# Dense attention's first key and query tiles placed among the branch tiles of the two-map attention, merged chunks stored one by one, buffers laid out anew

## The reference, cut to what matters

```
u = rms_norm(h)
qa, ka, va, qb, kb, vb, ga, gb = split(u @ w_in)
oa = rms_norm((softmax(q1 k1) - lam * softmax(q2 k2)) va)        # two-map attention, branch a
qh = axial_rope(rms_norm(qb)); kh = axial_rope(rms_norm(kb))     # dense attention, branch b
ob = softmax(qh kh) vb                                           # 8 query heads, 2 key heads
merged = sigmoid(ga) * (oa @ w_branch_a) + sigmoid(gb) * (ob @ w_branch_b)
h = h + merged @ w_out
```

## Time and profile before

| | us |
|---|---|
| median of 3 runs | 3543.96 (3541.33 to 3544.52) |
| the profiled execution, its own time | 3540.61 |
| its span, first to last instruction | 3538.8 |
| PE busy | 3312.3 (94% of the span) |
| DVE busy | 1410.5 (40%) |
| ACT busy | 1013.9 (29%) |
| POOL busy | 801.9 (23%) |
| PE, share of the chain that ended last | 52% |

### The profile page before, as it was taken

The page is one execution under the profiler, slowest core; times in us unless marked ns, Lnnn a source line. Parts: engine busy times, 40 slices in busy tenths (PEclk is TensorE's granted clock), DMA queues, the critical chain, the costliest instruction groups (busy, mean ns, idle before and its releaser), DMA issues.

```text
span 3538.8 us, 52696 instructions
## 1 busy us (share of the span) xinstructions
PE 3312.3 (94%) x20576; PEld 2907.5 (82%) x20576; DVE 1410.5 (40%) x2478; ACT 1013.9 (29%) x1873; POOL 801.9 (23%) x513
## 2 busy tenths in 40 slices
PE   7999988999999998999999889899999999879996
PEld 5677766888887887898989689889898999679996
DVE  4555543000002545666666630255545134432222
ACT  3433331000001213554555520145444210300001
POOL 3111133333332333122111123201000123012221
PEclk9999999999999998999999999999999999989998
DMA  4011122111112112000000001300000121458986
GB/s 148 31 31 31 31 73 84 48 46 45 46 46 96 48 48 91 19 19 21 24 20 19 13 24 47 109 17 25 27 25 19 53 98 59 171 194 307 316 309 238
DMA packets 75339, 275.50 MB, mean 78 GB/s; under 512 B 10736, under 2 KB 15600, under 8 KB 74400
## 3 DMA queue, kind: packets, MB, share of 16 engines
q1 hardware_dynamic: 67952, 234.08, 19.4%
q0 software_dynamic: 5632, 17.04, 2.0%
q10 hardware_dynamic: 1584, 22.07, 1.5%
HBM read 229.49 MB, written 38.34 MB: 76 GB/s over the span
## 4 chain that ended last, share of the span: by engine, by line
PE 52%; DVE 4%; issue 3%; ACT 1%; DMA 1%; POOL 0%; SPq 0%; DVEq 0%; ACTq 0%; POOLq 0%
PE PS L555 13%; PE PS L2875 7%; PE PS L2475 6%; PE PS L543 5%; PE PS L2661 3%; PE PS L2539 3%; PE PS L2905 3%; PE PS L2737 3%; PE PS L2506 3%; PE PS L2702 3%; PE PS L2685 0%; PE PS L2540 0%; PE PS L2819 0%; PE PS L2738 0%; DMA part_b<-raw_b 0%
## 5 line engine op out<-in xcount | busy, mean ns | idle before, releaser
L577 POOL CAST w_hi<-ring 128x1024 fp32r<-128x1024 f32 x174 | 182.9, 1051 | 1919.0 <-PE PS L555 772.4
L579 POOL TENSOR_TENSOR w_lo<-ring,w_hi 128x1024 fp32r<-128x1024 f32 x174 | 436.2, 2507 | 14.0
L555 PE MATMUL PS<-u_hi,w_hi 128*128 128x512 f32 (+1 forms) x1256 | 351.2, 371 | 17.6 <-DVE u_lo L509 7.7
L555 PE MATMUL PS<-u_lo,w_hi 128*128 128x512 f32 (+1 forms) x1256 | 350.9, 370 | 0.0
L555 PE MATMUL PS<-u_hi,w_lo 128*128 128x512 f32 (+1 forms) x1256 | 348.3, 369 | 0.0
L555 PEld LDWEIGHTS PS<-u_hi,w_hi 128*128 128x128 f32 x1256 | 228.2, 190 | 56.3 <-issue 12.7
L555 PEld LDWEIGHTS PS<-u_hi,w_lo 128*128 128x128 f32 x1256 | 228.3, 189 | 37.5
L555 PEld LDWEIGHTS PS<-u_lo,w_hi 128*128 128x128 f32 x1256 | 228.6, 189 | 35.5
L1726 ACT ACTIVATE EA<-EA,small_sb 128x1040 f32<-128x1040 f32 x144 | 166.7, 1158 | 211.0 <-DVE small_sb L2075 211.0
L1204 DVE TENSOR_TENSOR hid<-sq,PS 128x1024 f32 x22 | 26.9, 1221 | 457.9 <-PE PS L555 457.9
L2075 DVE CUSTOM_DVE_ANT_0 EA<-PS,biasH,low_a 128x1024 f32<-128x1024 f32 x128 | 163.6, 1278 | 68.1 <-PE PS L2506 62.7
(11 more groups left out here) (406 smaller groups left out, 6740.8 us busy)
## 6 DMA issues: line engine op xcount, KB each, us to landing
ring<-in_stream SPq DMA_DIRECT2D x174, 512.0 KB, 3.6
w_gate_sb<-in_w_gate SPq DMA_DIRECT2D x64, 512.0 KB, 6.4
w_up_sb<-in_w_up SPq DMA_DIRECT2D x64, 512.0 KB, 8.1
w_down_sb<-in_w_down SPq DMA_DIRECT2D x64, 512.0 KB
x_keep<-xT ACTq DMA_DIRECT2D x2, 4176.0 KB, 12.9
xT<-x_keep ACTq DMA_DIRECT2D x1, 4176.0 KB, 13.4
x2T<-x_keep ACTq DMA_DIRECT2D x1, 4176.0 KB, 13.7
x_keep<-x2T SPq DMA_DIRECT2D x1, 4176.0 KB, 15.1
```

Source lines behind the costliest of these rows:

```text
L555: last = mm(bank(to_bank, width), w[j][:, c, :], src[:, c, b * width:(b + 1) * width], start=(c == 0 and k == 0), stop=(c == KD - 1 and k ...
L577: pool.tensor_copy(w_hi[j][:, :, :], w_raw[j][:, :, :]).then_inc(S["w_rounded"], 1)
L579: pool.tensor_tensor(w_lo[j][:, :, :], w_raw[j][:, :, :], w_hi[j][:, :, :], ALU.subtract).then_inc(S["w_split"], 1)
```

## The change

**Order.** Branch a stops after branch tile 3 and gate tile 5 (`AHEAD = 4`). The tiles K and Q run there. Then come branch tile 4, the query sums, gate 6, branch 5, gate 7, branch 6, branch 7, and only then V. The stream's layout, the tile numbers and SP's queue follow that order. The loops on the three engines run over four chunks; the rest is written out.

**Stores.** `gated` writes its product in place, over `gate_a`. ACT stores each chunk (522 KB) by itself when it is done, and the sigmoid of gate d waits until chunk d-2 has landed. The last waits are for all 8 chunks.

**Buffers.** The tables, `raw_b`, `part_b`, the squares, `q_f`, `k_f`, `k_hi` and `k_lo` lie behind the operands of branch a, so they can be written while that runs. `q_hi`, `q_lo`, `vTb`, `EB`, `Vb` and `PTb` lie over those operands and are written after branch tile 7. The tables load early, when the turned output is out of its buffer. K's thirds go to banks 6, 7, 3, its sums to 4, 5, 4, Q's thirds to 0, 1, 2, and the first query sums to bank 7.

```diff
+AHEAD = 4
+FIRST0 = MG0 + 2 * AHEAD + 2
...
         def item_tile(g, x):
-            return B0 + g * ITEMS + x
+            return FIRST0 + x if g == 0 and x < VALUES else B0 + g * ITEMS + x
...  (SP)
-                pairs(A0 + 2, B0 + 2)
-                sp.wait_ge(S["w_used"], tile_done(B0 - 1))
+                pairs(A0 + 2, FIRST0 + 2)
+                sp.wait_ge(S["as_t"], 2 * (NT + 1))
                 sp.dma_start(cos[:, :], A["cos"]).then_inc(S["rope_ld"], 16)
                 sp.dma_start(sin[:, :], A["sin"]).then_inc(S["rope_ld"], 16)
+                for x in (KEYS, FIRST):
+                    swapped(0, x)
+                pairs(FIRST0 + 4, item_tile(0, VALUES) + 2)
...  (ACT)
-                act.wait_ge(S["mg_ma"], KD + CREDIT)
-                act.dma_start(m_keep, mergedT[:, :, :]).then_inc(S["m_st"], 16)
+                def keep(d, j):
+                    act.wait_ge(S["mg_ma"], d + 1 + CREDIT)
+                    act.dma_start(m_keep[:, bass.ds(d, 1), :].rearrange("p a n -> p (a n)"), gate_a[j][:, :]).then_inc(S["m_st"], 16)
+                def next_gate(d, j, late=0):
+                    keep(d - 2, j)
+                    act.wait_ge(S["m_st"], 16 * (d - 1))
+                    sigmoid(d, j, gate_tile(d, late), 0)
+                with act.Fori(1, AHEAD // 2 + 1) as i:
+                    for j in range(2):
+                        next_gate(2 * i + j, j)
                 for c in range(3):
                     wait_unit(0, KEYS, c)
-                    rope_raw(0, KEYS, c, c)
+                    rope_raw(0, KEYS, c, (6, 7, 3)[c])
                 for c in range(3):
-                    key_root(0, c, (6, 7, 6)[c])
+                    key_root(0, c, (4, 5, 4)[c])
                     wait_unit(0, FIRST, c)
-                    rope_raw(0, FIRST, c, 3 + c)
-                act.wait_ge(S["m_st"], 16)
+                    rope_raw(0, FIRST, c, c)
+                split_keys(0)
+                query_root(0, 0)
+                for d in range(AHEAD + 2, KD):
+                    next_gate(d, d % 2, 1)
+                keep(KD - 2, 0)
+                act.wait_ge(S["w_used"], tile_done(B0 + 1))
+                split_queries(0, 0)
+                keep(KD - 1, 1)
...  (DVE)
-                    dve.tensor_tensor(mergedT[...], thirds(gate_a[j][:, :]), banks(3, 3, CH), ALU.mult)
+                    dve.tensor_tensor(thirds(gate_a[j][:, :]), thirds(gate_a[j][:, :]), banks(3, 3, CH), ALU.mult)
...
                 query_recip(0, 0)
-                dve.wait_ge(S["m_st"], 16)
+                for d in range(AHEAD, KD - 1):
+                    gated(d, d % 2, branch_tile(d, 1))
+                gated(KD - 1, 1, B0 + 1)
                 lower_queries(0, 0)
                 meta_scores(0, 0)
+                scores_b(0)
+                dve.wait_ge(S["m_st"], 16 * KD)
...  (PE)
+                with pe.Fori(0, AHEAD) as d:
+                    branch_a(d, 0, branch_tile(d))
+                    gate_a_tile(d + 2)
+                pe.wait_ge(S["mg_ma"], AHEAD + CREDIT)
                 for c in range(3):
-                    whole_unit(0, KEYS, c, c)
-                pe.wait_ge(S["mg_ma"], KD + CREDIT)
+                    whole_unit(0, KEYS, c, (6, 7, 3)[c])
+                pe.wait_ge(S["mg_sa"], AHEAD + 2)
                 for c in range(3):
                     if c == 2:
                         pe.wait_ge(S["ob_ksd"], 1)
-                    key_sums(0, c, (6, 7, 6)[c])
-                    whole_unit(0, FIRST, c, 3 + c)
+                    key_sums(0, c, (4, 5, 4)[c])
+                    whole_unit(0, FIRST, c, c)
                 pe.wait_ge(S["ob_ksd"], 3)
+                branch_a(AHEAD, 0, branch_tile(AHEAD, 1))
+                query_sums(0, 0)
+                gate_a_tile(AHEAD + 2, 1)
+                for d in range(AHEAD + 1, KD - 1):
+                    branch_a(d, 0, branch_tile(d, 1))
+                    if d + 2 < KD:
+                        gate_a_tile(d + 2, 1)
+                branch_a(KD - 1, 1, B0 + 1)
+                pe.wait_ge(S["ob_sd"], 1)
                 for c in range(2):
                     whole_unit(0, VALUES, c, 6 + c)
-                query_sums(0, 0)
+                pe.wait_ge(S["mg_sa"], KD)
                 scores_b(0)
-                pe.wait_ge(S["ob_sd"], 1)
+                pe.wait_ge(S["mg_ma"], KD + CREDIT)
                 query_meta(0, 0)
                 whole_unit(0, VALUES, 2, 4)
                 scores_b(1)
```

More of the change, by code:

```diff
@@ L290, in build @@
         ob_end = o.at
+        q_hi = o.put("q_hi", [P, T2], F32R)
+        q_lo = o.put("q_lo", [P, T2], F32R)
+        vTb = o.put("vTb", [P, T2])
+        EB = [o.put(f"EB{j}", [P, T2]) for j in range(3)]
+        Vb = o.put("Vb", [P, NT, HB])
+        meta_b = [o.put(f"meta_b{j}", [P, NT + 1, META]) for j in range(2)]
+        low_b = [o.put(f"low_b{j}", [P, NT + 1]) for j in range(2)]
+        qm_hi, qm_lo = (o.put(n, [P, GROUP * META], F32R) for n in ("qm_hi", "qm_lo"))
+        Vb_meta = [o.put(f"Vb_meta{j}", [P, HB]) for j in range(2)]
+        PTb = [o.put(f"PTb{j}", [P, NT + 1, P]) for j in range(2)]
+        assert o.at <= early_at
+        o = Overlay(early_at, top)
+        cos = o.put("cos_sb", [P, T2])
+        sin = o.put("sin_sb", [P, T2])
         raw_b = [o.put(f"raw_b{j}", [P, CH]) for j in range(2)]
@@ L305, in build @@
         sq_m, qm_f = o.put("sq_m", [P, GROUP * META]), o.put("qm_f", [P, GROUP * META])
[L306 to L313, removed]
         ob_hi = at("ob_hi", [P, HEADS, TP], uT_at, F32R)
@@ L632, in wait_taken, with gate_tile, branch_tile @@
                 pe.wait_ge(S["conv_y"], 2 * of + half + 1)
[L634 to L640, removed]
+        def gate_tile(d, late=0):
+            return MG0 + 2 * d - 1 + 2 * late
+        def branch_tile(d, late=0):
+            return MG0 + 2 * d + 2 + 2 * late
         def tile_done(n):
@@ L1526, in pairs, with swapped @@
                                 also(n - first)
-                pairs(A0 + 2, B0 + 2)
-                sp.wait_ge(S["w_used"], tile_done(B0 - 1))
+                def swapped(g, x):
+                    n = item_tile(g, x)
+                    sp.wait_ge(S["w_split"], n + 1)
+                    load(sp, n + 2, n % 2)
+                    for c in range(0 if x == VALUES else 3):
+                        k = rope_chunk(g, x, c)
+                        w = width_of(c)
+                        sp.wait_ge(S["ob_raw"], 2 * k + 1)
+                        if k >= 2:
+                            sp.wait_ge(S["ob_q"], k - 1)
+                        for r in range(0, P, 32):
+                            sp.dma_start(part_b[k % 2][r:r + 32, 0:w], raw_b[k % 2][r ^ 32:(r ^ 32) + 32, 0:w]).then_inc(S[f"ob_sw{k % 2}"], 16)
+                pairs(A0 + 2, FIRST0 + 2)
+                sp.wait_ge(S["as_t"], 2 * (NT + 1))
                 sp.dma_start(cos[:, :], A["cos"]).then_inc(S["rope_ld"], 16)
                 sp.dma_start(sin[:, :], A["sin"]).then_inc(S["rope_ld"], 16)
+                for x in (KEYS, FIRST):
+                    swapped(0, x)
+                pairs(FIRST0 + 4, item_tile(0, VALUES) + 2)
                 for g in range(KV):
[L1535 to L1546, removed]
+                    for x in range(0 if g else VALUES, ITEMS):
+                        swapped(g, x)
                 pairs(GB0 + 2, GB0 + 4)
                 sp.wait_ge(S["bb_ob"], NB)
-                sp.wait_ge(S["m_st"], 16)
+                sp.wait_ge(S["m_st"], 16 * KD)
                 def merged(c):
@@ L2144, in _ @@
                     dve.memset(part[:, :, T2:TP].bitcast(F32), 0.0).then_inc(S["pad_set"], 1)
[L2146 to L2157, removed]
                 def rope(g, x, c):
@@ L2259, in result_b, with gated @@
                         dve.tensor_copy(obT[:, GROUP * g:GROUP * (g + 1), T1:T2], bank(7, GROUP * META).rearrange("p (h n) -> p h n", n=META)).then_inc(S["bb_ob"], 1)
+                def gated(d, j, n):
+                    dve.wait_ge(S["mg_sa"], d + 1)
+                    dve.wait_ge(S["w_used"], tile_done(n))
+                    dve.tensor_tensor(thirds(gate_a[j][:, :]), thirds(gate_a[j][:, :]), banks(3, 3, CH), ALU.mult).then_inc(S["mg_ma"], 1)
+                with dve.Fori(0, AHEAD // 2) as i:
+                    for j in range(2):
+                        gated(2 * i + j, j, branch_tile(2 * i + j))
+                dve.wait_ge(S["rope_ld"], 32)
                 for c in range(3):
@@ L2673, in query_sums @@
                     for t in range(NT):
-                        last = mm(bank(5, 1, 256 + t), sq_b[:, t * P:(t + 1) * P], ones[:, 0:1], start=True, stop=True)
+                        last = mm(bank(5, 1, 256 + t) if g or j else bank(7, 1, 400 + t), sq_b[:, t * P:(t + 1) * P], ones[:, 0:1], start=True, stop=True)
                     if j == GROUP - 1:
@@ L2947, in layout @@
     late += [w_in2[GA]] + [t for d in range(KD - 1) for t in (w_in2[GA + d + 1], w_a[d])] + [w_a[KD - 1]]
```

(4 more changed lines are left out.)

27 lines of the change are left out of this document (6 added, 21 removed).

## The result

The kernel after takes 3521.78 us (median of 4 runs, 3520.29 to 3522.62) against 3543.12 us (4 runs), a ratio of 0.9946 with a 95% interval of 0.9934 to 0.9958. The forecast was 3522.4. The span of the profiled execution went from 3538.8 to 3518.5 us, 20.3 less.

A forecast was written before the change was run, and what follows sets the result against it. PE bounds the kernel; its idle and low-clock time around K, Q and V can be won. The stretch's terms sum to 41.84 us against 63.47, so 3543.96 - 21.6 = 3522.4 us; 8-in-10 range 3519 to 3531.

The forecast's parts named there:

- The sum: First matmul of K to second scores, branch tiles left out: 41.84 us instead of 63.47, so 21.6 us go.
- K and Q: PE's matmuls of K and Q with the key sums: 26.07 us less the idle 1.13, 24.94 us.
- the wait for the roots: PE's wait for the three key roots, now before branch tile 4: 0.5 us, bounds 0 and 3.
- the query sums: PE's query sums in the stretch: 1.84 us.
- V to the second scores: V's 72 matmuls 11.45 us, first scores 1.40, meta scores 1.71, at full clock.
- The key chain: Swaps, adds and roots of K's thirds, with POOL's split in the middle: third root at 24.9 to 25.0 us.
- `q_lo`: PE's 2.75 us wait goes: `q_lo` needs 5 us after branch tile 7, V's two thirds cover 7.6.
- gates and stores: Sigmoids wait for the chunk store two before: 18.9 us of cover, a chunk lands in 4.5, nothing counted.
- Slow swaps: Rival: key swaps stay slow without the store, only 2.75 and 4.9 us go, 3536.3 us; chance 0.08.
- The chain as DVE's: Rival before branch tile 4: PE waits 3 to 4 us, 3525 to 3527 us; within the forecast's 0.85.
- The gate ring: Rival: store landings of 24 us delay sigmoids, 5 us at each of gates 2 to 7, 3552 us; chance 0.02.
- No gain: Rival: the time won is given back where the clock or a DMA sets the end; chance 0.03.

The follow-up runs named there:

- kernel 2: Kernel after plus one store of 4176 KB on ACT's queue about 1 us after K starts, tables still early: 3530.03 us, ratio 0.9961.
- Kernels 2 to 4: kernel 2, kernel 4 and, between them, the kernel after with both tables loaded at K's start, without the large store: 3519.96 us, ratio 0.9940.
- kernel 4: Kernel after with both the 4176 KB store beside K and the two tables loaded at K's start: 3536.02 us, ratio 0.9987.
- kernel 5: Kernel after with a 4176 KB store ahead of each of chunk stores 0, 1, 2, 4 and 5: 3522.7 us, ratio 0.9947.
- kernel 1: Kernel before, in its old order and layout, with products in place and eight chunks stored one by one: 3530.83 us, ratio 0.9968.
- kernel 10: Kernel after with half of the large store, 2088 KB in one DMA, beside K: 3520.87 us, ratio 0.9941.
- kernel 8: Kernel after with ACT's split of next queries and keys moved before the exponential, and branch tile 7 in banks 0 to 2: 3494.27 us, ratio 0.9871.

## Why the prediction was right

**The sum.** 41.84 us forecast, 41.45 measured. K and Q 24.94 and 24.66; the wait for the roots 0.5 and 0.28 (0.45 with the start of the next matmul); the query sums 1.84 and 1.7; V to the second scores 14.56 and 14.64. Nothing of it was mis-sized by more than 0.3 us. That the median came within 0.6 us of the forecast is more than the sum can claim: it was taken from 3543.96, the four runs of the kernel before scatter by 3 us, and the traced gain is 22.0 us in the stretch and 20.3 in the span.

**The key chain**, counted from the start of K: first add done at 9.4 forecast and 9.5 measured; POOL's split lengthened the second add to 15.3 and 15.8 (2.60 us for a work of 0.52, and the multiply ahead of it 1.05); third add 16.9 and 17.4; third root 24.9 to 25.0 and 25.1. Two small errors cancel here: the chain was 0.5 us late at the third add, and from there to the root it took 7.65 us, where the prediction had 8.05 (10.55 less 2.5). It is a close race: the wait is small because PE's 24.7 us and the chain's 25.1 happen to agree, and microseconds more on a swap are paid, as in kernel 2.

**The two causes.** The prediction left open what held the swap, the store or SP's loads. Kernels 2 to 4 show that the store has to be there, and that the loads make it worse only then. In kernel 2 the swap had SP's queue to itself, and its first DMA of 43.5 KB still landed with the end of the store on ACT's queue. The Trainium skill says in DMA: Bandwidth & Descriptors, section Queues, rings and completion order, that a DMA engine takes packets in turn from the queues that have work. By that rule the swap would have passed most of the store; the measurement differs, and it decides. Why the swap was held is not shown by any run.

**`q_lo`, gates and stores.** `q_lo` was done at 2281.8, 2.7 us after the end of branch tile 7 where 5 were allowed, with V under way until 2286.8. DVE did not wait for POOL there: product and `q_lo` took 1.24 us each, and it was POOL's split beside `q_lo` that was long, 3.47 us instead of 2.4. The product of chunk 4 came 3.6 us after its tile (2.3 forecast: POOL's split held a small DVE instruction for 1.45), long before PE asked. A chunk landed in 2.7 us, not 4.5 (2.6 to 4.1, where the prediction looked for 4 to 6 as a sign), and kernel 5 shows that 14 would do.

**The rivals.** Slow swaps: priced at 3536.3, and kernel 4, which brings their cause back, took 3536.0. The chain as DVE's: POOL's split fell on it once and cost 2.6 us (0.53 on the multiply, 2.08 on the add), which the sum had in it. The gate ring: not seen at 14 us. No gain: nothing was given back by a new wait; the 2 us between the 22.0 of the stretch and the 20.3 of the span lie in code that did not change, and part of them in the choice of the end point.

**What the prediction did not say** is how the 21.6 us divide. The new order, which is most of the diff, brings 5.5 us of the stretch; the small stores bring 16.5. In the times of the runs it is 7 to 9 us for the order and 12 to 14 for the stores (kernels 1 and 4).

## What to carry to other kernels

A large transfer is not free because nobody waits for it: ask which small transfer is issued while it is under way, and who waits for that one. Send the data as they come, before the stretch that needs quick copies. A wait of 2.5 us that the profile calls "issue" and that recurs at the same place of a loop is worth a look at what ended just before it: here it was another engine's order of work, and moving the split of the next tile ahead of an exponential won as much as the whole change. Count with such a wait also the matmuls at the low clock that can follow it.

## What the runs showed of the hardware that was not expected

- A small DMA on one queue did not pass a large store on the other: 43.5 KB took 7.5 us instead of 1.9 and landed with the end of 4176 KB (kernel 2), and a table of 520 KB took 15.0 instead of 5.0 us (kernel 4). Where the store ended 2.2 us after the small DMA's issue, that took 2.4 us (kernel 10).
- Issuing eight DMAs of 522 KB back to back took ACT 7.98 us, while its single issues of that size in the kernel after took 0.34 to 0.37.
- The same wait of PE was followed by the low clock in one place and not in another. After waits of 2.5 us in the woven loop the next 3 us ran at 0.51 to 0.68 four times of seven in the kernel after, and at 1.00 the other three; after 2.68 us they ran at 0.51 (kernel 1). A wait of 1.4 us before branch tile 7 was followed by 1.00 in every trace that has it, one of 1.45 us in the woven loop by 1.00 in the kernel after and by 0.56 in kernel 8.
